# Attention values and key/value compression: products on different PSUM partitions issued in turn instead of one partition range after the other

## What is computed

```python
def compress(tok, pe, w):                      # for keys and for values
    blk = tok[:, tok_idx] + pe[None, None, :, None, :]   # 15 windows of CMP_LEN = 32 tokens
    blk = blk.transpose(0, 1, 3, 2, 4).reshape(B, n_cmp, G, CMP_LEN * dh)
    return blk @ w
kc = compress(k_cmp_tok, pe_k, w_cmp_k)
vc = compress(v_cmp_tok, pe_v, w_cmp_v)
...
o_c = einsum('bgrqc,bcgd->bqgrd', p_c, vc)     # compressed branch
o_s = einsum('bgrqn,bgqnd->bqgrd', p_s, v_g)   # selected branch
o_w = einsum('bgrqk,bkgd->bqgrd', p_w, v_w)    # window branch
o_nsa = bg[:, :, 0] * o_c + bg[:, :, 1] * o_s + bg[:, :, 2] * o_w
```

## Time and profile before

| what | value |
|---|---|
| median of 3 runs | 2088.76 us (2088.62 to 2089.74) |
| the profiled execution's own time | 2087.42 us |
| its span | 2085.7 us |
| PE busy | 1932.7 us, 93% of the span |
| DVE busy | 1059.0 us, 51% |
| ACT busy | 504.5 us, 24% |
| mean granted TensorE clock | 0.982 |

### The profile page before, as it was taken

The page is one execution under the profiler, slowest core; times in us unless marked ns, Lnnn a source line. Parts: engine busy times, 40 slices in busy tenths (PEclk is TensorE's granted clock), DMA queues, the critical chain, the costliest instruction groups (busy, mean ns, idle before and its releaser), DMA issues.

```text
span 2085.7 us, 20851 instructions
## 1 busy us (share of the span) xinstructions
PE 1932.7 (93%) x8000; PEld 1420.7 (68%) x8000; DVE 1059.0 (51%) x2577; ACT 504.5 (24%) x1222; POOL 325.2 (16%) x333
## 2 busy tenths in 40 slices
PE   6999999999999999999999999998987888887877
PEld 5877788888886788888888777785443443443332
DVE  6995675401796422001201423216877767767755
ACT  2133321111114222110011445212222222222223
POOL 1000001000000000000000000004444444444441
PEclk9999999999999999999999999999999999999899
DMA  9614369844441143449642222527999999999997
GB/s 398 247 42 161 132 261 422 354 155 149 156 189 61 63 165 141 153 150 224 211 186 81 96 96 81 202 101 326 421 422 421 421 421 421 421 421 421 416 421 290
DMA packets 72435, 517.39 MB, mean 248 GB/s; under 512 B 8208, under 2 KB 8464, under 8 KB 11664
## 3 DMA queue, kind: packets, MB, share of 16 engines
q0 software_dynamic: 46384, 330.85, 39.5%
q1 hardware_dynamic: 25952, 185.21, 23.7%
HBM read 510.78 MB, written 5.24 MB: 247 GB/s over the span
## 4 chain that ended last, share of the span: by engine, by line
PE 62%; DMA 20%; DVE 14%; ACT 2%; issue 1%; POOL 0%; DVEq 0%; SPq 0%; POOLq 0%; ACTq 0%
DMA region<-in_peer_uv,small 18%; PE pj L609 14%; PE pj L861 10%; PE pj L876 8%; PE st L1135 5%; DVE region L1663 5%; PE pj L807 5%; DVE region L2058 2%; PE pj L622 2%; PE pj L905 1%; PE pj L1106 1%; PE pj L1006 1%; PE st L947 1%; DMA ring<-in_ring_w 1%; DVE region L1690 1%
## 5 line engine op out<-in xcount | busy, mean ns | idle before, releaser
L1135 PE MATMUL st<-region 128*128 128x512 f32 x940 | 458.4, 637 | 105.3 <-ACT region L1499 105.3
L1135 PEld LDWEIGHTS st<-region 128*128 128x128 f32 x940 | 184.1, 203 | 359.7 <-issue 193.4
L609 PE MATMUL pj<-hT,ring 128*128 128x256 f32 x1760 | 385.0, 380 | 1.0 <-ACT region L1318 1.0
L2058 DVE CUSTOM_DVE_ANT_0 region<-region 128x1024 f32<-128x1024 f32 x235 | 287.4, 1224 | 164.4 <-DMA region<-in_peer_uv,small 162.1
L609 PEld LDWEIGHTS pj<-hT,ring 128*128 128x128 f32 x1760 | 332.6, 190 | 47.1 <-ACT region L1318 1.8
L516 POOL DMA_INDIRECT region<-in_peer_uv,small x235 | 261.2, 1111 | 388.4 <-PE st L1135 318.5
L861 PE MATMUL pj<-region,ring 128*128 128x256 f32 x1024 | 222.0, 379 | 0.7 <-DMA ring<-in_ring_w 0.7
L861 PEld LDWEIGHTS pj<-region,ring 128*128 128x128 f32 x1024 | 194.3, 190 | 28.2 <-DMA ring<-in_ring_w 1.1
L1663 DVE SCALAR_TENSOR_TENSOR region<-region,pc 128x255 f32<-128x255 f32 (+19 forms) x528 | 202.7, 470 | 0.0
L1499 ACT ACTIVATE region<-ident,small 128x128 f32<-128x128 f32 x256 | 89.4, 395 | 456.8 <-DVE small L2066 455.1
L1614 DVE TENSOR_TENSOR tmp<-xT,hT 128x256 f32<-128x256 f32 x32 | 13.6, 426 | 360.1 <-ACT hT L1214 360.1
(11 more groups left out here) (376 smaller groups left out, 2074.3 us busy)
## 6 DMA issues: line engine op xcount, KB each, us to landing
ring<-in_ring_w SPq DMA_DIRECT2D x157, 1024.0 KB, 4.8
region<-in_ada_rest POOLq DMA_DIRECT2D x40, 1024.0 KB, 12.4
region<-in_ada_first SPq DMA_DIRECT2D x8, 1024.0 KB, 18.7
region<-in_wqkv SPq DMA_DIRECT2D x2, 3072.0 KB, 12.2
region<-in_wcmp POOLq DMA_DIRECT2D x2, 2048.0 KB, 9.6
bias_dram<-region POOLq DMA_DIRECT2D x1, 4096.0 KB, 45.9
region<-in_w_o POOLq DMA_DIRECT2D x4, 1024.0 KB, 6.4
region<-in_peer_uv,small POOLq DMA_INDIRECT x235, 16.7
```

Of the source, the lines that this page charges most:

```text
L609: i = nc.tensor.matmul(b[:, m, :], w[:, k, P * m:P * m + P], hT[:, k, :], start=(k == 0), stop=(k == CT - 1))
L1135: i = nc.tensor.matmul(acc[:, u % 2, 512 * hf:512 * hf + 512], diag[:, m % NDIAG, :], uv[m % NBUF][:, D + 512 * hf:D + 512 * hf + 512], st ...
L2058: nc.vector.tensor_tensor_reduce(row, row, h_tok[:, u % 2, :], 1.0, 0.0, ALU.mult, ALU.add, dots[:, u, k:k + 1]).then_inc(sem("u_used"), 1)
```

## The change

In `values`, both parities of heads are issued in turn: for every m and j first the product for partitions 0 to 63, then the one for partitions 64 to 127, and at the end the two products of the compressed branch. In the compression, keys and values are issued in turn for every window position, and the sum of the values now stands on partitions 32 to 61 of the same PSUM bank instead of in other columns of partitions 0 to 29. So `cmp_rows` has 128 columns on partitions 0 to 29 and 32 to 61, ACT fills it with two copies in place of one, and the second transpose reads partitions 32 to 61 and writes to `ms[0]` instead of `ms[1]`. The products themselves, their sizes and their number are as before.

```diff
--- before.py
+++ after.py
@@ -311,7 +311,7 @@
         bgate = small_piece(448, 96).rearrange("p (s n) -> p s n", s=2)
         has = sb("has", [P, 1])
         cmpc = small_piece(384, 60).rearrange("p (m g c) -> p m g c", m=2, g=2)
-        cmp_rows = small_piece(3072, 256, 2 * NCMP)
+        cmp_rows = small_piece(3072, P, 64)
         vc = small_piece(544, 256, NCMP).rearrange("p (g e) -> p g e", g=2)
         pcmp = small_piece(800, 120).rearrange("p (b r c) -> p b r c", b=2, r=R)
         pcmpT = small_piece(920, 512, NCMP).rearrange("p (r t) -> p r t", r=R)
@@ -911,9 +911,9 @@
 
             pe.wait_ge(sem("wcmp_in"), 32)
             pe.wait_ge(sem("blk_ready"), 1)
-            for m in range(2):
-                for i_ in range(CMP_LEN):
-                    i = nc.tensor.matmul(ms[1][0:2 * NCMP, 0, P * m:P * m + P], blk[:, m, :, :, i_], wcmp[m][:, i_, :],
+            for i_ in range(CMP_LEN):
+                for m in range(2):
+                    i = nc.tensor.matmul(ms[1][32 * m:32 * m + 2 * NCMP, 0, 0:P], blk[:, m, :, :, i_], wcmp[m][:, i_, :],
                                          start=(i_ == 0), stop=(i_ == CMP_LEN - 1))
             i.then_inc(sem("cmp_made"), 1)
             pe.wait_ge(sem("wgn_in"), 16)
@@ -928,7 +928,8 @@
                 if m == 0:
                     pe.wait_ge(sem("cmp_kept"), 1)
                     for n in range(2):
-                        t = nc.tensor.transpose(ms[1][:, 0, 32 * n:32 * n + 2 * NCMP], cmp_rows[:, P * n:P * n + P], ident[0:2 * NCMP, 0:2 * NCMP])
+                        lo, hi = 32 * n, 32 * n + 2 * NCMP
+                        t = nc.tensor.transpose(ms[1 - n][:, 0, lo:hi], cmp_rows[lo:hi, :], ident[lo:hi, lo:hi])
                     t.then_inc(sem("cmp_made"), 1)
             i.then_inc(sem("bgate_made"), 1)
 
@@ -999,11 +1000,12 @@
                     return
                 nb = NCMP if s else NCMP // 2
                 gp, lo = g // 2, HD * (g % 2)
-                for hf in range(2):
-                    o = b[HD * hf:HD * hf + HD, 0, :].rearrange("p (a t) -> p a t", a=2)
-                    for m in range(2):
-                        for j in range(s + 1):
+                halves = [b[HD * hf:HD * hf + HD, 0, :].rearrange("p (a t) -> p a t", a=2) for hf in range(2)]
+                for m in range(2):
+                    for j in range(s + 1):
+                        for hf, o in enumerate(halves):
                             nc.tensor.matmul(o, v2[:, m, j, HD * g:HD * g + HD], probsT[:, m, j, hf:R:2, :], start=(m == 0 and j == 0), stop=False)
+                for hf, o in enumerate(halves):
                     i = nc.tensor.matmul(o, vc[0:nb, gp, lo:lo + HD], pcmpT[0:nb, hf:R:2, :], start=False, stop=True)
                 i.then_inc(sem("o_made"), 1)
 
@@ -1364,10 +1366,12 @@
             drain2(kselT[:, 1], "kwin")
             drain2(v2[:, 1], "vwin")
             act.wait_ge(sem("cmp_made"), 1)
-            nc.scalar.copy(cmp_rows, ms[1][0:2 * NCMP, 0, :]).then_inc(sem("cmp_kept"), 1)
+            for n in range(2):
+                i = nc.scalar.copy(cmp_rows[32 * n:32 * n + 2 * NCMP, :], ms[1][32 * n:32 * n + 2 * NCMP, 0, 0:P])
+            i.then_inc(sem("cmp_kept"), 1)
             act.wait_ge(sem("cmp_made"), 2)
             nc.scalar.copy(cmpc[:, 0].rearrange("p g c -> p (g c)"), ms[1][:, 0, 0:2 * NCMP])
-            nc.scalar.copy(cmpc[:, 1].rearrange("p g c -> p (g c)"), ms[1][:, 0, 32:32 + 2 * NCMP]).then_inc(sem("cmp_kept"), 1)
+            nc.scalar.copy(cmpc[:, 1].rearrange("p g c -> p (g c)"), ms[0][:, 0, 32:32 + 2 * NCMP]).then_inc(sem("cmp_kept"), 1)
             drain2(qxT[:, 0:2, :], "qx0")
             act.wait_ge(sem("bgate_made"), 1)
             nc.scalar.activation(bgate[:, :, :].rearrange("p s n -> p (s n)"), pj[bank_of()][:, 0, 0:96], ACT.Sigmoid).then_inc(sem("proj_drained"), 1)
```

## The result

The changed kernel takes 2065.92 us (median of 4 runs, 2064.28 to 2066.55) against 2088.69 us before, a ratio of 0.989 with a 95% interval of 0.9877 to 0.9904: 22.8 us less. Forecast were 14.1 us less and a range down to 2068.4 us.

What follows compares the result with a forecast made beforehand. PE alone was taken to bound compression and attention units. Savings of 10.1 us in `values` (2.2 us of term 1 included) and 4.0 in the compression, 14.1 off 2088.8, gave 2074.7 us; range 2068.4 to 2087.2.

Steps and rivals of the forecast that it cites:

- What bounds the kernel: Compression and attention units wait for PE alone, busy 93% of the span; what PE saves there should reach the end.
- Term 1: In `values`, two borders of stationary shape fewer per unit, 0.09 + 0.05 us each, over eight units: 2.2 us saved.
- Term 2: In `values` and compression, neighbouring products on different output partitions may run at once; bounded from nothing saved to halved pairs.
- overlap, but weight loads in order: Case taken: ranges overlap, each range change exposes its load; 10.1 us in `values`, 4.0 in the compression; chance 0.38.
- The upper bound: B's first matmul starts with A's second: pairs take 0.432 us instead of 0.864 in `values`, 0.218 instead of 0.436 in compression.
- Full overlap: Rival: loads for the other range run ahead of waiting matmuls in both places; 19.6 us saved, 2069.2 us, chance 0.30.
- no overlap: Rival: steps stay steady in both places and only the fewer shape borders save, 2.2 us, 2086.6 us; chance 0.10.
- loads in the open: Rival: no overlap, each range change in `values` and compression shows its load; 3.2 us more, 2092.0 us, chance 0.06.
- the array emptied at each change: Rival: a range change costs what a shape change does, 0.14 us at 111 places; 13.3 us more, 2102.1 us, chance 0.10.
- Only one place overlapping: Rival: only `values` or only the compression overlaps; 10 or 4 us gained, 2079 to 2085 us, chance 0.06.
- What lies beside it: ACT's two copies, the transposes, DMA and the turns waiting for the softmax have slack and cost nothing.

Runs made afterwards that it cites:

- same-partition run: Kernel before with only the compression's keys and values issued in turn, both sums on partitions 0 to 29 in two banks: 2088.65 us, ratio 1.0.

## Why the prediction was wrong

- **What bounds the kernel**: right. What PE saved in both places came out at the end; turns and expert stage brought no new wait.
- **Term 1, fewer borders of shape**: consistent, but never seen alone. The s = 1 unit is 2.77 us, of which three borders remain at 0.31, 0.31 and 0.3 us.
- **Term 2, neighbours on different partitions**: this is the step that failed, by its size. Of the 14.1 us it had 11.9 (14.1 less the 2.2 of term 1); by the same reckoning it measured 20.6 (22.8 less 2.2). Of its cases the prediction took "overlap, but weight loads in order". The rows had shown a load never before the matmul in front of it, and I read that as the order of issue. It was no more than the wait of one range for itself. With two ranges, loads start 0.01 us apart, and no 0.05 us stands in the open behind the first step: pairs take 0.43 and 0.22 us, not 0.53 and 0.31.
- **The upper bound, and with it the range**: wrong as well. Full overlap was priced with B's first matmul beside A's second (3.19 and 2.32 us for a unit, 19.6 us in all). B's first runs beside A's first: 2.77 and 1.90 us, 0.42 us less in each unit, which are the two steps of 0.216 us that the tails of its two runs don't have. 8 x 0.42 = 3.4 us, and 19.6 + 3.4 = 23.0, against 22.8 measured. I had bounded an unknown by keeping the order of issue, which no row showed to hold between ranges. An upper bound without it would have been half of every run, 10 of the 20 and 6 of the 12 matmuls of a unit and 64 of the compression's 128: 4 x (10 + 6) x 0.216 + 64 x 0.109 = 20.8 us, and with term 1's 2.2 us 23.0.
- **The rivals**: no overlap, loads in the open and the array emptied at each change are excluded, since L916 halves and the steps of each range stay at 0.109 us. Only one place overlapping is excluded too, since each change alone gained. The Trainium skill ("TensorE: Matmul & The Clock Gate", Part 3) was the better guide on the start of neighbouring tiles, some 4 ns apart; the trace shows 0.01 us. The prediction read that as its case of full overlap, 19.6 us; taken at its word it gives the 23.0 us above, by my estimate from the rows. The Trainium skill's statement in the same part that matmuls never start out of order does not hold in these traces: blocks of four took 8.5 us where strict order allows 12.2. Nor does the Trainium skill's rule there that a load overlaps a running matmul only where the row groups differ: here all have 128 rows, and the first loads, 0.14 us together, lie inside the 0.34 us of the first two matmuls. That a change of tile alone does not drain ("TensorEngine Tiling (Array Packing)", Key Properties), the trace agrees with: from the second step on, no step of a range in L916 is above 0.11 us.
- **What lies beside it**: right for ACT's second copy (the same-partition run has it and takes the time of before) and for the turns.

## What to carry to other kernels

Where a stationary tile has 64 or 32 columns or fewer, several independent sums, or parts of one sum, can go to different ranges of 64 or 32 PSUM partitions and run side by side: two ranges halved a stretch, four quartered it, and a sum split in four pays with one or two more products to add the parts. The products need not alternate strictly; two of one range in a row lost nothing, four lost a part. It pays only where the inputs are all there and PE is what the end waits for, which the chain of waits tells: the scores behind the gate sums of layer 1 began 5.6 us earlier, while of sums whose inputs came one by one only the tail was saved, 1.46 us. Where PE is not what the end waits for, a shorter stretch can cost: in layer 0 PE stood idle for most of the time it had saved, and ran the next matmuls at half clock.

## What the runs showed of the hardware

- Four ranges with 30-column tiles run at the full rate each: 128 matmuls of 0.273 us in 3.76 us, loads included.
- Output on the same partitions in another bank gives no overlap at all: 13.9 us in either order.
- The granted clock fell to 1.2 GHz for 3.4 us in the attention units in some executions and in none of others of the same program, at a price of 1.7 us. A profiled span can be off by that much, so a comparison of two spans needs the clock of each stretch beside it.
- Of one range's waiting matmuls PE passed three and not a fourth: in blocks of four products, the other range's first matmul started with the fifth of eight. With four ranges in turn the last range's first matmul also had three waiting ones in front (one of each other range), and started at once.
- In idle times of PE of 2.69 and 6.91 us the granted clock fell to half, for 3.4 and 10.2 us. It also fell once with no idle time in the 4.5 us before, as the stretch behind unit 0 shows.
- What stays open is whether the limit of three counts the waiting matmuls of one range or of all. No run has blocks of three, or four ranges in blocks.
